# Prompt attention woven into the sample attention, V pages requested ahead of K pages, in a two-layer hybrid decoder step

## The chip, the cores and the metric

One NeuronCore of a Trainium2 chip runs the whole step as one program. The metric is device time in microseconds, the median of several executions. One further execution was profiled; all rows come from it.

## The reference, cut to what matters

A prompt of 512 tokens and a sample group of 8 sequences with 8 new tokens each (576 tokens, T) pass two decoder layers of width 1024, all in float32. Layer 0 mixes tokens by trailing mean pooling (256 channels) and by forgetting attention (12 heads of 64), layer 1 by gated spatial mixing and retention; each has an MLP of 4096 behind. The change touches layer 0's mixer alone:

```python
# prompt: causal, over its own 512 rows, logits biased by differences of the summed log gates
sc = einsum('bqhd,bkhd->bhqk', qb, k) * scale + cb[..., :, None] - cum[..., None, :]
p = softmax(where(kpos <= qpos, sc, -inf)); o = einsum('bhqk,bkhd->bqhd', p, v)
# samples: 8 queries of each sequence over 4096 past rows (32 pages of 128, by page_table) and 8 new ones
s_past = einsum('bqhd,bkhd->bhqk', q, k_past) * scale + g[..., :, None] + suffix[..., None, :]
p = softmax(concatenate([s_past, s_new])); o = p_past @ v_past + p_new @ v
```

The past keys and values are 256 pages of K and 256 of V, 384 KiB each, 201 MB in all. The pooling's new history rows, K, V and the log gates of the new tokens are outputs too.

## The kernel before

Activations lie with channels on the partitions, tokens along the free dimension (`big`, `xn`, `h`). Each engine has its own instruction list, in program order, and they meet by semaphores; SP issues the loads of weights and pages, GpSimd (POOL) those of small tables and the stores.

**Order of layer 0.** After the first norm come the ten column pairs of the input projection (`pairs("in", 0)`, a scheme of seven products, `seven`). Then TensorE transposes the cached log gates (`sfxT`) and sums them up (`sfx`), takes the new tokens' gates (`logfT`, `cum`, `cumT`), and turns K and V of the new tokens into rows (`knat`, `vnat`), which POOL stores (`k_stored`, `v_stored`). Then the **prompt attention**: 48 steps, 12 heads of 4 query blocks. Step n: `score` (L974, L975) of block i against i + 1 key blocks, with the gate as an extra row of staged queries and keys (`qz`, `kz`, filled by ScalarE's `queries` and small SP loads); VectorE's `maximum`, ScalarE's exponential, VectorE's `divisors` (a diagonal matrix of reciprocals), TensorE's `turn` (L985), ScalarE's copy, per head `weigh` (L996) and VectorE's `head_out`. It is pipelined over four score banks and three turning banks. POOL makes the pooling differences meanwhile. After it the pool outputs, then the sample attention.

**Sample attention.** The 32 pages of a sequence go in 4 groups of 8: 32 groups g. K pages go into a ring of 12 slots (4-page blocks), V pages into one of 8. VectorE transposes each K page in place (`turn_page`, L1898). `score_group(g)` (L1047) is 224 small matmuls that fill four banks; it starts when all eight pages are turned. VectorE takes the maximum (`shift_group`, L1913), ScalarE the exponential (L1462), TensorE transposes the probabilities (`turn_probs`), ScalarE copies them (L1477), TensorE weighs V pages 0 to 3 (`weigh_page`, L1069), and pages 4 to 7 behind the next score block. In TensorE's list, for each g:

```python
score_group(g)
if g: 
    for p in range(GP // 2, GP): weigh_page(g - 1, p)
turn_probs(g)
for p in range(GP // 2): weigh_page(g, p)
```

VectorE's list for g: `turn_pages(g + 1, 0..2)`, `shift_group(g)`, page 3, `add_out(g - 1)`, the bias, pages 4 to 7. SP's list runs through pages n in fours: K pages n to n+3 (L540, waiting for `scored` >= (n - 12) // 8 + 1 from page 12 on), then V pages n-8 to n-5 (L545, each waiting for `v_page_used` >= page - 7 from page 8 on). Two batches of page numbers are read into registers ahead of each such eight (L528).

The new tokens' own scores, `score_new`, `turn_new`, `weigh_new`, come once per sequence, and `turn_out`, `place_out` bring its result into `xn`. After the last group follows the output projection (`pairs("out", 0)`), whose two weight units were loaded into `wring` during the input projection.

Of the kernel before, what the change touches and what calls it, by code (L numbers as in the profile page):

```python
# [57 lines left out]
for _n, _k in PARAMS:  # L58
# [6 lines left out]
STAGES = [("x", KD), ("norm0", 1), ("logf", 1), ("sfxT", 12), ("logfT", 1), ("sfx", 6),  # L65
          ("cum", 1), ("knat", 5), ("cumT", 1), ("vnat", 5), ("hist", 2), ("g96", 1),
# [158 lines left out]
def hybrid_step(nc, I, O, where0, where1, decay_step):  # L225
    ctx = ExitStack()
    with ctx:
# [29 lines left out]
        kTn = sb("kTn", [TS, FOX])  # L257
# [23 lines left out]
        def bankB(s, n=TS, rows=P):  # L281
# [7 lines left out]
        vs = bigf[:, at0 + 3072:at0 + 3840]  # L289
        q4 = bigf[:, at0 + 3840:at0 + 5376].rearrange("p (n t) -> p n t", n=2 * H)  # L290
        qcur = bigf[:, at0 + 5376:at0 + 6912].rearrange("p (e c i f n) -> p e c i f n", e=2, c=CG, i=HC, f=2)
        key_bias, qgate = sbias[:, 0:TS], sbias[:, TS:TS + NB]
        at1 = EV_V * T
        es = [bigf[:, at1 + 1536 + 368 * n:at1 + 1536 + 368 * (n + 1)].rearrange("p (a b t) -> p a b t", a=2, b=NB)
              for n in range(2)]
        hstage = bigf[0:NB * HIST, at0 + 6408:at0 + 6664]
        hcopy = bigf[:, at1 + 2528:at1 + 2768].rearrange("p (a t) -> p a t", a=2)
        hout = bigf[0:NB * HIST, at1 + 2768:at1 + 3024]
        hout_p = bigf[0:HIST, at1 + 3024:at1 + 3280]
# [3 lines left out]
        probs = work[:, 9216:10240]  # L303
        pTs = work[:, 10240:11264].rearrange("p (g r) -> p g r", g=GP)
        bias_nat = work[:, 11264:11520].rearrange("p (g n) -> p g n", g=GP)
        bias_T = work[:, 11520:12032].rearrange("p (e n) -> p e n", e=2)
        out_acc = work[:, 12032:12416].rearrange("p (e n) -> p e n", e=2)
        v_ring = bigf[:, EV_Q * T:EV_Q * T + VSLOTS * FOX].rearrange("p (s n) -> p s n", s=VSLOTS)
        at3 = EV_Q * T + VSLOTS * FOX
        probs_new = bigf[:, at3:at3 + NB * TS].rearrange("p (b t) -> p b t", b=NB)  # L310
        pTn = bigf[0:TS, at3 + NB * TS:at3 + NB * TS + P]
        ostage = bigf[:, at1 + 1136:at1 + 1328]
        lg = work[:, 0:3072].rearrange("p (a s h) -> p a s h", a=2, h=H)
        kstage = work[:, 0:3840].rearrange("p (t n) -> p t n", t=NT + 1)
# [3 lines left out]
        vn0 = work[:, W2:W2 + NT * FOX].rearrange("p (t n) -> p t n", t=NT)  # L318
# [6 lines left out]
            .rearrange("p (s n) -> p s n", s=4)  # L325
        ngate = rstd[0:H, 0:SEQ]

        KZ = W1 + 1024 + 2 * EXT + 4 * P
        kz = [xn[:, KD - 1, 0:SEQ], work[:, KZ:KZ + SEQ]]

        def stat(b, n):
# [1895 lines left out]
```

## Time and profile before

| | |
|---|---|
| median of 3 runs (lowest, highest) | 2286.21 us (2284.81, 2288.41) |
| the profiled execution: time, span | 2289.08 us, 2287.2 us |
| busy: PE, VectorE, ScalarE, GpSimd | 87%, 47%, 15%, 9% of the span |
| input projection and what precedes it | 0 to 185.2 us |
| gates, K and V rows | 185.2 to 240.6 us |
| prompt attention and pool outputs | 240.6 to 358.7 us |
| sample attention: first page requested, block 0 done, block 31 done | 358.75, 380.8, 922.2 us |
| output projection begins | 936 us |
| read from memory, written | 309.2 MB, 8.55 MB |

Busy shares are means over stages with different limits, so they say little about one stage; the stage is cut out by windows, and in it one asks which wait ends last. In rows of the timeline "idle before <-releaser" is the time that the engine stood idle before the instruction, and what ended it.

### The profile page before, as it was taken

How to read it: one execution, taken by the hardware profiler on the slowest of the kernel's cores; microseconds unless marked ns; L12 is line 12 of the kernel's file. 1: busy time of each engine (PE TensorE's matmuls, PEld its weight loads, DVE VectorE, ACT ScalarE, POOL GpSimd, SP SyncE). 2: the span in 40 equal slices, each digit the busy share in tenths (PEclk: the TensorE clock that was granted, in tenths of full speed). 3: DMA queues.
4: the chain of work that ended last, by engine and by line, in shares of the span. 5: the costliest groups of instructions: out<-in, count | busy, mean ns of one | idle time of the engine just before them, and what ended most of it. 6: DMA issues, size and time to landing. Idle time of an engine off the chain costs nothing.

```text
span 2287.2 us, 40891 instructions
## 1 busy us (share of the span) xinstructions
PE 1981.6 (87%) x16723; PEld 1487.8 (65%) x16723; DVE 1064.5 (47%) x1915; ACT 354.2 (15%) x817; POOL 197.5 (9%) x266
## 2 busy tenths in 40 slices
PE   6999885666766666889999999999997899999996
PEld 4777663444444444667777777677775677777774
DVE  5331855565665565453334444232456533344443
ACT  2002451111111111112221000111011022210002
POOL 1000500000000000100001222100001100002221
PEclk9999997888788898999999999999898999999998
DMA  4221106999999999312222222222111222222221
GB/s 162 74 74 38 63 2 225 340 373 357 372 367 355 357 384 367 119 37 74 74 74 90 93 76 74 74 74 74 39 32 56 74 74 74 74 74 74 74 74 42
DMA packets 127990, 320.42 MB, mean 140 GB/s; under 512 B 10236, under 2 KB 10514, under 8 KB 127678
## 3 DMA queue, kind: packets, MB, share of 16 engines
q1 hardware_dynamic: 124258, 304.67, 36.4%
q0 software_dynamic: 3296, 12.98, 1.7%
q8 instruction: 134, 2.20, 0.4%
q14 instruction: 50, 0.41, 0.1%
q10 hardware_dynamic: 252, 0.16, 0.0%
HBM read 309.20 MB, written 8.55 MB: 139 GB/s over the span
## 4 chain that ended last, share of the span: by engine, by line
PE 76%; DVE 8%; DMA 6%; issue 5%; SPq 4%; ACT 1%; ACTq 0%; DVEq 0%
PE ps L847 49%; PE ps L1047 7%; DMA work<-in_cache_k 5%; DVE work L1898 3%; PE ps L1161 3%; PE ps L1162 3%; SPq L540 2%; PE ps L769 1%; PE ps L770 1%; PE ps L996 1%; SPq L545 1%; PE ps L798 1%; PE ps L799 1%; SPq L528 1%; PE ps L1069 1%
## 5 line engine op out<-in xcount | busy, mean ns | idle before, releaser
L1898 DVE STREAM_TRANSPOSE work<-work 128x768 f32<-128x768 f32 x256 | 245.2, 971 | 160.9 <-DMA work<-in_cache_k 160.1
L847 PE MATMUL ps<-xn,wring 128*128 128x288 f32 x1104 | 295.5, 411 | 20.0 <-DVE xn L1617 15.7
L847 PE MATMUL ps<-work 128*128 128x288 f32 x1152 | 296.5, 411 | 12.4 <-DVE work L1664 7.8
L847 PEld LDWEIGHTS ps<-work 128*128 128x128 f32 x1152 | 221.7, 193 | 75.6 <-issue 13.7
L847 PEld LDWEIGHTS ps<-xn,wring 128*128 128x128 f32 x1104 | 212.4, 193 | 80.7 <-issue 20.0
L847 PE MATMUL ps<-big,wring 128*128 128x288 f32 x944 | 251.4, 410 | 7.6 <-DVE big L2172 7.6
L1047 PE MATMUL ps<-work,big 32*32 32x256 f32 x6144 | 165.4, 471 | 92.2 <-DVE work L1898 61.6
L847 PEld LDWEIGHTS ps<-big,wring 128*128 128x128 f32 x944 | 181.0, 192 | 58.7 <-DVE big L2172 8.5
L1047 PEld LDWEIGHTS ps<-work,big 32*32 32x32 f32 x6144 | 113.9, 115 | 136.4 <-DVE work L1898 74.3
L1691 DVE TENSOR_TENSOR work<-ps,work 128x288 f32<-128x288 f32 x72 | 33.0, 458 | 320.1 <-PE ps L847 320.1
L702 POOL TENSOR_TENSOR h<-h,xn 128x288 f32<-128x288 f32 x96 | 106.1, 1108 | 812.4 <-DVE xn L1698 697.6
L1069 PE MATMUL ps<-big,work 128*32 128x192 f32 x2048 | 126.5, 394 | 48.1 <-ACT work L1477 32.0
L847 PE MATMUL ps<-work,wring 128*128 128x288 f32 x576 | 151.4, 406 | 0.0
L1069 PEld LDWEIGHTS ps<-big,work 128*32 128x32 f32 x2048 | 70.1, 128 | 97.8 <-ACT work L1477 39.3
L847 PEld LDWEIGHTS ps<-work,wring 128*128 128x128 f32 x576 | 109.4, 190 | 30.2
L1383 ACT ACTIVATE work<-ps 128x288 f32<-128x288 f32 x72 | 29.6, 411 | 622.0 <-PE ps L847 622.0
L847 PE MATMUL ps<-big,work 128*128 128x288 f32 x448 | 116.2, 406 | 0.0
L1462 ACT ACTIVATE work<-ps,stats 128x1024 f32<-128x1024 f32 x32 | 35.7, 1114 | 441.9 <-DVE stats L1915 441.9
L847 PEld LDWEIGHTS ps<-big,work 128*128 128x128 f32 x448 | 85.1, 190 | 23.5
L847 PE MATMUL ps<-xn,work 128*128 128x288 f32 x368 | 96.7, 406 | 0.0
L1161 PE MATMUL ps<-xn,wring 128*128 128x288 f32 x256 | 83.1, 406 | 0.0
L1162 PE MATMUL ps<-xn,wring 128*128 128x288 f32 x256 | 83.0, 406 | 0.0
(348 smaller groups left out, 2345.2 us busy)
## 6 DMA issues: line engine op xcount, KB each, us to landing
work<-in_cache_k SPq DMA_DIRECT2D x256, 384.0 KB, 5.9
big<-in_cache_v SPq DMA_DIRECT2D x256, 384.0 KB, 7.5
wring<-in_w_up SPq DMA_DIRECT2D x16, 2048.0 KB, 7.6
wring<-in_w_down SPq DMA_DIRECT2D x16, 2048.0 KB, 7.8
wring<-in_w_in_odd SPq DMA_DIRECT2D x6, 2048.0 KB, 8.1
wring<-in_w_in_even SPq DMA_DIRECT2D x5, 2048.0 KB, 9.1
wring<-in_w_out_even SPq DMA_DIRECT2D x2, 2048.0 KB, 8.4
wring<-in_w_out_odd SPq DMA_DIRECT2D x2, 2048.0 KB, 7.8
```

Of the source, the lines that this page charges most:

```text
L528: _, ids = nc.values_load_multi_w_load_instructions(ptab[0:1, n:n + 4], engines=[mybir.EngineType.SP], min_val=0, max_val=NPHYS - 1)
L540: sp.dma_start(k_ring[:, k_slot(n), :], rows_of("cache_k", page)).then_inc(k_in[k_slot(n)], 16)
L702: pool.tensor_tensor(hs[name], hs[name], xouts[kind, layer][:, g % 2, a, :], ALU.add)\
L847: last = mm(bank, w[:, k, :], x[:, k, :], start=k == 0 and not onto, stop=k == 3, skip_group_check=onto)
L1047: last = mm(ps[32 * c:32 * c + 32, 4 + q, 0:256], w, x, start=(n == 0), stop=(n == 2 * HC))
L1069: last = mm(ps[32 * c:32 * c + 32, 3, 0:HC * D], pTs[:, place(g, p), 32 * c:32 * c + 32], v_ring[:, n % VSLOTS, HC * D * c:HC * D * (c + 1 ...
L1161: mm(bankA(s, TH), w, xn[:, k, 0:TH], start=(k == 0), stop=(k == KD - 1))
L1162: last = mm(bankB(s, TH), w, xn[:, k, TH:T], start=(k == 0), stop=(k == KD - 1))
L1383: act_f(sums_at(g)[2][:, g % 2, :], ps[:, 4 * (g % 2), 0:TH], ACT.Copy).then_inc(sem("p1_copied"), 1)
L1462: act_f(probs.rearrange("p (g q k) -> p q g k", g=GP, q=4), ps[:, 4:8, 0:256].rearrange("p q (g k) -> p q g k", g=GP), ACT.Exp, bias=shift ...
L1691: ins = tt(u2, bank[1], first[:, g % 2, :], ALU.add)
L1898: nc.vector.transpose(x, x).then_inc(sem("k_turned"), 1)
```

## The change

- **The prompt's 48 steps are spread over the sample groups 0 to 23**, two a group, with the tail in group 24 (`prompt_step(2 * g)` between weighing V pages 4 to 7 and `turn_probs`, `prompt_step(2 * g + 1)` at the end of the group). One score bank, one turning bank, two exponential buffers take the place of four, three and four. Queries and keys are read from `big` directly, and the gate is a matmul of its own with a broadcast column of the identity; `queries` and the SP loads of the gate rows are gone. The queries are scaled in place by ScalarE during the input projection, and `place_queries` moves there.
- **Pages are requested from the end of `sfx` on.** In SP's list four V pages stand ahead of each four K pages. V page 0 waits for the K rows' stores and the turned new keys, since the V ring now lies in `wring`. The output projection's weights go into `big`, behind the last K page and a wait for the last prompt head.
- **Pooling moves ahead**: the history transposes come before the first norm's products, POOL's pooling runs under the input projection and writes its differences in place (`big`), the history outputs come right after the projection, the group matmuls (`pooled`) ahead of `g96`. ScalarE waits for `pool_d_ready` before it copies the gates' transposes.
- **TensorE waits for `v_stored` ahead of `score_new(0)`**; before it waited for it ahead of the same call, but behind the prompt attention. `score_group` also waits for `outputs_placed`. `stage_queries`, `score_new`, `shift_new` come one group earlier (GS - 3), `turn_new`, `weigh_new`, `start_out` half a group to a group earlier.

```diff
@@ SP
-            unit("out0", 0)
-            unit("out0", 1)
             sp.wait_ge(sem("ptab_in"), 16)
-            sp.wait_ge(sem("ngate_ready"), 1)
...
-            for hd in range(H):
...
-                sp.dma_start(kz[hd % 2][r:r + 1, :], ngate[hd:hd + 1, :]).then_inc(sem(f"gates_in_{hd % 2}"), 16)
-            sp.wait_ge(sem("fox_prompt_done"), H)
+            wait_emptied(sp, FIRST["sfx"] + 6)
...
             def v_page(n, page):
+                if n == 0:
+                    sp.wait_ge(sem("k_stored"), 80)
+                    sp.wait_ge(sem("new_keys_turned"), 1)
...
             for n in range(GP, NB * PAGES, 4):
                 k_ids, v_ids = page_ids(n), page_ids(n - GP)
                 for m in range(4):
+                    v_page(n - GP + m, v_ids[m])
+                for m in range(4):
                     k_page(n + m, k_ids[m])
-                for m in range(4):
-                    v_page(n - GP + m, v_ids[m])
+            sp.wait_ge(sem("fox_prompt_done"), H)
+            unit("out0", 0)
+            unit("out0", 1)
@@ TensorE
+            pe.wait_ge(sem("v_stored"), 32)
+            gates = rstd[:, 0:SEQ]
             def score(n):
...
+                if n:
+                    pe.wait_ge(sem("probs_made"), n)
+                w, r = (i + 1) * P, slice(64 * (hd % 2), 64 * (hd % 2) + 64)
+                mm(ps[:, 0, 0:w], big[r, EV_Q + hd // 2, i * P:w], big[r, EV_K + hd // 2, 0:w], start=True, stop=False)
+                mm(ps[:, 0, 0:w], ident[:, hd:hd + 1].broadcast_to([P, P]), gates[:, 0:w], start=False, stop=False)
+                mm(ps[:, 0, i * P:w], ident, cst("mask"), start=False, stop=True).then_inc(sem("scores_made"), 1)
...
+            def prompt_step(n):
+                if n >= NT + 1 and (n - 1) % NT == 0 and n <= NSTEP + 1:
+                    weigh((n - 1) // NT - 1)
+                if 1 <= n <= NSTEP:
+                    turn(n - 1)
+                if n < NSTEP:
+                    score(n)
...
             for g in range(NG):
                 b, new = g // GS, g // GS + 1
                 score_group(g)
+                if g % GS == GS - 2 and new < NB:
+                    turn_new(new)
                 if g:
                     for p in range(GP // 2, GP):
                         weigh_page(g - 1, p)
...
+                prompt_step(2 * g)
                 turn_probs(g)
...
                 for p in range(GP // 2):
                     weigh_page(g, p)
...
                 if g % GS == 0 and b:
                     turn_out(b - 1)
+                prompt_step(2 * g + 1)
@@ ScalarE
             for g in range(NG):
+                if 1 <= 2 * g - 1 < NSTEP:
+                    exp_prompt(2 * g - 1)
+                if 0 <= 2 * g - 2 < NSTEP:
+                    take_turned(2 * g - 2)
                 exp_group(g)
+                if 1 <= 2 * g - 1 < NSTEP:
+                    take_turned(2 * g - 1)
                 take_probs(g)
+                if 2 * g < NSTEP:
+                    exp_prompt(2 * g)
@@ VectorE
                 turn_pages(g + 1, range(0, 3))
+                if 1 <= 2 * g - 1 < NSTEP:
+                    divisors(2 * g - 1)
                 shift_group(g)
...
                 if g:
                     add_out(g - 1)
...
+                if 2 * g < NSTEP:
+                    maximum(2 * g)
+                if g % 2 == 1 and g >= 3 and g // 2 - 1 < H:
+                    head_out(g // 2 - 1)
+                turn_pages(g + 1, range(3, 4))
                 if g + 1 < NG:
                     turn_bias(g + 1)
...
+                turn_pages(g + 1, range(4, 5))
+                if 2 * g < NSTEP:
+                    divisors(2 * g)
+                turn_pages(g + 1, range(5, 8))
...
                 if g % GS == 0 and b:
                     place_out(b - 1)
+                if 2 * g + 1 < NSTEP:
+                    maximum(2 * g + 1)
```

## Rows read from the trace of the kernel before

**Rows 1.** The page, DMA share in tenths and GB/s in 40 equal slices.

```profile
DMA  4221106999999999312222222222111222222221
GB/s 162 74 74 38 63 2 225 340 373 357 372 367 355 357 384 367 119 37 74 74 74 90 93 76 74 74 74 74 39 32 56 74 74 74 74 74 74 74 74 42
```

**Rows 2.** Windows: us, busy PE, PEld, DVE, ACT, POOL, clock, DMA share, GB/s.

```profile
185.20:240.60 55.40, 49.91 (x204) 39.31 (x204) 14.91 (x36) 16.89 (x37) 9.68 (x16) 0.93 0.24 86
240.60:358.70 118.10, 102.99 (x538) 76.82 (x539) 72.67 (x226) 58.26 (x167) 23.96 (x31) 0.96 0.03 9
...
380.80:922.20 541.40, 353.71 (x9561) 230.82 (x9565) 325.02 (x541) 77.52 (x138) 11.65 (x60) 0.85 0.97 360
922.20:936.00 13.80, 7.55 (x108) 4.23 (x107) 6.74 (x20) 2.41 (x4) 0.00 (x0) 0.87 0.36 116
```

**Rows 3.** DMA queues, 381 to 922 us: packets, MB, share of 16 engines.

```profile
q1 hardware_dynamic: 70848, 193.49, 95.8%
```

**Rows 4.** Timeline, 374 to 390 us: start us, us, engine, line, operation.

```profile
379.80 0.99 PE L1047 MATMUL ps<-work,c 32*32 32x256 f32 x27
...
380.97 1.88 SPq L540 DMA_DIRECT2D work<-in_cache_k  x4
...
386.00 2.79 PE L1069 MATMUL ps<-big,work 128*32 128x192 f32 x32 [1.11 <-ACT work L1477]
387.13 1.97 DVE L1898 STREAM_TRANSPOSE work<-work 128x768 f32<-128x768 f32 x2 [0.47 <-DMA work<-in_cache_k]
...
389.15 1.24 PE L1047 MATMUL ps<-work,big 32*32 32x256 f32 x43 [0.36 <-DVE work L1898]
```

**Rows 5.** Timeline, 920 to 932 us, the end of the stage.

```profile
921.23 0.40 PE L1047 MATMUL ps<-work,big 32*32 32x256 f32 x1 [2.94 <-issue]
...
921.23 0.97 PE L1047 MATMUL ps<-work,c 32*32 32x256 f32 x32
...
930.67 0.53 PE L1069 MATMUL ps<-big,work 128*32 128x192 f32 x8 [0.41 <-DMA big<-in_cache_v]
```

**Rows 6.** SP queue's own waits, 381 to 922 us: us, times, longest.

```profile
SPq L540 <- PE ps L1047: 55.0, 24, 4.9
```

**Rows 7.** Line 540, requests of 380.9 to 382.9 us, time to landing.

```profile
DMA to landing us min/median/max: 2.9/4.6/5.6
```

**Rows 8.** Line 1047 alone, 374 to 922.2 us, columns as in Rows 2.

```profile
374.00:922.20 548.20, 191.42 (x7168) 131.28 (x7168) 0.85 0.96 358
```

**Rows 9.** Waits, 374 to 922.2 us: us in total, times, longest.

```profile
PE ps L1047 <- issue: 53.8, 24, 3.8
```

**Rows 10.** Lines, 240 to 358 us: busy us, mean ns, idle before.

```profile
L985 PE MATMUL ps<-work 128*128 128x128 f32 x240 | 36.7, 285 | 12.4 <-issue 8.0 <-DVE work L1850 3.4 <-ACT work L1442 0.8
...
L1850 DVE TENSOR_SCALAR work<-c,hstat 128x128 f32<-128x128 f32 x48 | 17.9, 372 | 1.8 <-DVE hstat L1849 0.2
L974 PE MATMUL ps<-work 128*128 128x128 f32 (+3 forms) x48 | 17.4, 444 | 0.0
```

**Rows 11.** Stretch of 386 to 388 us, columns as in Rows 2.

```profile
386.00:388.00 2.00, 2.00 (x28) 1.27 (x32) 1.53 (x2) 0.00 (x0) 0.00 (x0) 0.50 0.95 376
```

**Rows 12.** Timeline, three moments between 224 and 363 us.

```profile
224.22 1.08 ACT L1402 ACTIVATE big<-ps 128x512 f32<-128x512 f32 x1 [0.63 <-PE ps L922]
...
237.27 0.79 POOL L619 DMA_DIRECT2D out_v_prompt<-work  x1 [4.16 <-DVE work L1793]
...
237.84 0.45 DVE L1807 COPY big<-ps 128x120 f32<-128x120 f32 x2
...
362.75 0.83 PE L1082 MATMUL ps<-kTn,big 32*32 32x8 f32 x48 [3.31 <-DVE big L1890]
```

**Rows 13.** All DMA issues: KB each, median us to landing.

```profile
out_v_prompt<-work POOLq DMA_DIRECT2D x1, 1536.0 KB, 5.8
```

**Rows 14.** Line 1842, all of the run: ns min/median/max.

```profile
L1842 DVE SCALAR_TENSOR_TENSOR hstat<-hstat,cumn x48: 219/220/1877, 242.6 to 347.5; 128x1 f32<-128x1 f32 x48
```

**Rows 15.** Timeline of SP's queue, 150 to 230 us.

```profile
157.65 27.53 SPq L504 DMA_DIRECT2D wring<-in_w_out_even  x2
```

More of the change, by code:

```diff
@@ L484, in unit @@
                 u = UFIRST[stage] + j
-                if u >= 2:
+                if u >= 2 and stage != "out0":
                     for name, n, per in WEIGHTS:
@@ L816, in _ @@
             pe.wait_ge(sem("params_ready"), 1)
+            pe.wait_ge(sem("hist_in"), 16)
+            for a in range(2):
+                s = slot("hist", a)
+                open_block(FIRST["hist"] + a)
+                tr(ps[:, 2 * s, 0:NB * HIST], hstage[:, a * P:(a + 1) * P], ident[0:NB * HIST, 0:NB * HIST])\
+                    .then_inc(block_in, 1)
             s = slot("logf")
@@ L894, in _ @@
             pe.wait_ge(sem("c11_out_in"), c11_before(last_in + 1, "in"))
+            s = slot("hist_out")
+            for a in range(2):
+                tr(ps[0:NB * HIST, 2 * s + a, 0:P], hcopy[:, a, :], ident)
+                last = tr(ps[0:HIST, 2 * s + a, P:2 * P], hcopy_p[:, a, :], ident)
+            last.then_inc(block_in, 1)
             pe.wait_ge(sem("lg_in"), 32)
@@ L1716, in first_weight_sums, with place_queries, under_in @@
                     weight_sum(pairs_of(kind, layer)[0], name)
+            def place_queries(n):
+                a, f, q = n // 8, n // 4 % 2, n % 4
+                at = 64 * a + 32 * f
+                cp(q4[32 * q:32 * q + 32].rearrange("p (n a f) t -> p a f n t", a=2, f=2)[:, a, f],
+                   big[at:at + 32, EV_Q:EV_Q + HB, SEQ:T])
+            def under_in(g):
+                if g == 0:
+                    dve.wait_ge(sem("mixed"), MIX["C21"])
+                    for a in range(2):
+                        own(cp(es[0][:, a, :, HIST:HIST + NS], big[:, a, SEQ:T].rearrange("p (b s) -> p b s", b=NB)))
+                        cp(hcopy[:, a, :].rearrange("p (b t) -> p b t", b=NB), es[0][:, a, :, NS:NS + HIST])
+                    cp(hcopy_p, big[:, 0:2, SEQ - HIST:SEQ]).then_inc(sem("ext_ready"), 1)
+                if 5 <= g < 9:
+                    dve.wait_ge(sem("queries_scaled"), 3)
+                    for n in range(4):
+                        place_queries(4 * (g - 5) + n)
             def pairs(every, last=None):
@@ L1756, in _ @@
             first_weight_sums("in", 0)
+            for a in range(2):
+                s = drained("hist", a)
+                cp(es[0][:, a, :, 0:HIST], ps[:, 2 * s, 0:NB * HIST].rearrange("p (b t) -> p b t", b=NB))\
+                    .then_inc(out_of["vector"], 1)
             norm(0, PROW["norm_mix"], 0)
@@ L1770, in _ @@
             act_sum(0, "T4")
-            pairs(pairs_of("in", 0))
+            pairs(pairs_of("in", 0), under_in)
             dve.wait_ge(sem("c11_out_in"), c11_before(pairs_of("in", 0)[-1] + 1, "in"))
+            nc.vector.memset(rstd[:, :], 0.0).then_inc(sem("gates_zeroed"), 1)
+            s = drained("hist_out", 0)
+            for a in range(2):
+                cp(hout[:, a * P:(a + 1) * P], ps[0:NB * HIST, 2 * s + a, 0:P])
+                last = cp(hout_p[:, a * P:(a + 1) * P], ps[0:HIST, 2 * s + a, P:2 * P])
+            last.then_inc(out_of["vector"], 1)
+            wait_emptied(dve, FIRST["hist_out"] + 1)
+            dve.sem_inc(sem("hist_out_ready"), 1)
             dve.wait_ge(sem("log1p_ready"), 1)
@@ L1930, in shift_new @@
                 x = probs_new[:, b, NS * b:NS * b + NS]
-                own(tt(x, new_psum[:, 0:NS], key_bias[:, NS * b:NS * b + NS], ALU.add))
+                own(tt(x, ps[:, 2, 320:320 + NS], key_bias[:, NS * b:NS * b + NS], ALU.add))
                 own(nc.vector.reduce_max(neg_max(b, 0), x, AX.X, negate=True))
```

377 lines of the change are left out of this document (144 added, 233 removed).

## The prediction, made before the changed kernel was run

> **What bounds the kernel now.** I read the page first. Its DMA row is at 9 tenths over slices 8 to 16 of 40 and at 2 almost everywhere else [rows 1]. That names one stage in which memory is the limit: the sample attention, which streams 512 cache pages of 384 KiB. So I cut the span into stages. The prompt attention, 240.6 to 358.7 us, moves 9 GB/s. The sample attention between its first and its last finished score block, 380.8 to 922.2 us, moves 360 GB/s at a DMA share of 0.97 [rows 2], 95.8% of it the SP queue's packets [rows 3]. The two do not overlap: one stage has no traffic, the next has little else. That is what interleaving could win, at most about 118 us.
>
> The second question is whether the pages come at 360 GB/s whatever the order of the requests. One group is 16 pages (6.29 MB) and takes (922.20 - 380.79) / 31 = 17.46 us [rows 4, 5]. At 360 GB/s 16 pages take 17.47 us, so the rate sets it. But SP also waits 55.0 us in 24 places for `scored`, the end of a score block [rows 6]: there is a closed loop (scores of group g end, K pages are requested, land, are transposed, scores of g+1 run), and its slack is small. One turn of this loop from an empty queue is visible, because DMA ran dry before the first block ended: block 0 ends at 380.79, SP requests four K pages at 380.97, they land 2.9 to 5.6 us after their requests [rows 7], DVE turns the last one by 389.10, block 1 starts at 389.15 [rows 4]. That is 8.36 us from one block's end to the next one's start. A block itself takes (191.42 busy + 53.8 idle inside it) / 32 = 7.66 us [rows 8, 9]. Loop from empty: 8.36 + 7.66 = 16.0 us, against 17.46. So the present order leaves 1.4 us a group, which shows as requests queued. This is the number on which the change turns.
>
> **What the change does to the loop.** The new SP order puts four V pages ahead of each four K pages. In steady state the V pages ahead of the K half that group g+1 lacks are the second half of group g. Their ring slots come free only when `weigh_page(g-1, 4..7)` runs, which TensorE does right after score block g. So these requests can't be sent early: when block g ends, SP sits at a V request, sends four V, then the four K. The loop gains four pages. A page is 393 KB; at 360 GB/s 1.09 us, so 4.3 us, and about 0.4 us until the first page is weighed (32 records take 2.79 us at the lower clock [rows 4]). Gap 8.36 + 4.3 + 0.4 = 13.1 us; period 13.1 + 7.66 = 20.7 us. This exceeds 17.5 us, so the queue runs empty each turn and no backlog hides it. The second halves (V of g+1, K of g+2) go out at about 8 us and are through by 20 us; they just don't add. From both sides: not below the rate's 17.5 us; above, the four K pages from idle came 1.4 us apart (from 380.97 + 2.9 = 383.9 to about 388.1), and four more at that pace are 5.6 us: 22.0 us. I take 20.7, since that spacing fell in the first microseconds after idle, when little was under way.
>
> The Trainium skill (DMA: Bandwidth & Descriptors, Bandwidth) puts the limit of a core from memory at about 358 GB/s; the trace's 360 agrees. By that rule alone the order of requests is free and the period stays 17.5 us; that is the first rival below.
>
> **Prompt work inside the loop** (two steps a group, groups 0 to 23). TensorE: the prompt stage's PE busy time is 102.99 us [rows 2]; over 24 groups 4.3 us. The gates are now a matmul of their own over the score's width, 48 of them at the 444 ns of a score matmul [rows 10] or somewhat more (the records come in pairs): 0.9 to 1.8 us a group. The sample stage has 353.71 / 31 = 11.4 us busy a group [rows 2]. Together 17 us of a 20.7 us period: it fits, but little is free. Step 2g lies between the V weighing and `turn_probs`, where TensorE waits for the maximum and the exponential: hidden at the full clock. Step 2g+1 must end before block g+1. It waits for `divisors(2g)`, which VectorE now does behind `turn_page` 4, so behind a landing at about 9 us: the step ends at 11.5 to 13 us, abreast of the pages. VectorE: `divisors` (372 ns [rows 10] and a reciprocal) stands between transposes of the last pages and delays them by 0.5 us, the rest is done while it waits for pages. When a block stalls and the granted clock drops to 0.5, as at 386 us [rows 11], weighing and step 2g take twice as long. I take 0.5 us a group for both: period 21.2 us. In seven groups the next block also waits for `place_out` (about 0.6 us).
>
> Sum over the 31 periods: the first has no V slot to wait for (18.9 us), 23 at 21.2 = 487.6, 7 at 20.7 = 144.9, 7 x 0.6 = 4.2: 655.6 us against 541.4. **+114 us.**
>
> **The start.** The anchor is `score_new(0)`, at 362.75 us before [rows 12]. It now waits for `v_stored`. The V store is issued at 237.27 us [rows 12] and lands in 5.8 us [rows 13] with no other traffic. Before it come now the output transposes of the history (four 128x128 matmuls, with 285 ns each [rows 10] 1.1 us), two history copies ahead of the first norm (0.45 us [rows 12]), and the pooling on GpSimd, which moves under the input projection. Beside it a VectorE instruction of 220 ns once took 1.88 us [rows 14]; between 0 and 6 us in all, I take 2. The store also runs beside the first K and V pages, now requested from about 227 us (the suffix sums are copied out at 225.3 [rows 12]): I double its 5.8 us. 237.3 + 3.6 + 11.6 = 252.5, so **-110 to -111 us** (bounds -116 without contention, -106 with more). The Trainium skill (DMA: Bandwidth & Descriptors, Queues, rings and completion order) says that each DMA engine serves its queues in turn by packets; by that rule the store gets half the engines' time, the same doubling; no row here shows it. Block 0 then follows 18 us later as before (380.8 - 362.75): its pages are long there. Pooling, its matmuls and scaling, the query scaling on ScalarE and `place_queries` lie under the projection, TensorE's stage, or under the wait for the store: nothing; without that cover a few us.
>
> **The end.** The two weight units of the output projection (4 MiB, 11.6 us at 360 GB/s) were loaded at 157.65 us [rows 15]; now they stand between the last K and the last eight V pages. After block 30: 8 pages, 4 MiB, 8 pages, that is 26.7 pages, the last landing near 0.6 + 2.9 + 25.7 x 1.09 = 31.5 us, or 10.8 us after block 31 ends. Before, the last weighing started 8.5 us after it (930.67 - 922.20) [rows 5]. **+3 us** with its spread. The stages behind are unchanged.
>
> **Sum.** The profiled execution has 2289.1 us: -111 + 114 + 3 = +6, so 2295; it lies 2.9 above the median, so **2293 us** in the runs' terms: the hidden prompt attention is given back almost exactly by the loop.
>
> **Rivals.**
> *A. The rate hides the order.* If the V slots come free early enough, or landings overlap more, the period stays 17.5 us and only the start counts: 2286 - 111 + 3 = 2178 us. For it: share 0.97 and the match with 360 GB/s. Against it: `weigh_page(g-1, 4..7)` is behind block g in TensorE's own order, and the loop from empty has 1.4 us of slack for 4.7. Chance 0.10.
> *B. Score blocks get shorter.* 53.8 of their time is idle put down to issue [rows 9], and clock is lost after such stalls. If TensorE, kept busy or waiting longer ahead of a block, runs it in 191.42 / 32 = 6.0 us, periods are 19.5 and 19.1 us: 602 us, +60, 2286 - 111 + 60 + 3 = 2238 us. For it: the idle time lies in 24 places of 32 blocks, so some blocks run without. Against: the last block still waited 2.94 us [rows 5], after more waiting than the others. Chance 0.20.
> *C. TensorE becomes the bound,* the other side. 17 us of work with three waits in series (exponential, copy, `divisors`) at a lower clock: if step 2g+1 ends at 15.3 us instead of 13, it decides (from 13.6 us on). Period 23 us in 24 groups: 697 us, +155, 2286 - 111 + 155 + 3 = 2333 us. Chance 0.15.
> *Main case,* 0.55: 2270 to 2318 us (a period half a us shorter or longer is 16 us).
>
> **How the numbers follow.** What a measurement here can tell from no change is 0.2%, 4.6 us: 2281.6 to 2290.8 is the same. Faster: A, B and 0.07 of the main case, 0.37. Same: 0.11. Slower: C and 0.37 of the main case, 0.52. Signs of both kinds hold much, so the range is wide: 2235 to 2335 leaves out A and the far parts of B and C, 0.2 together. The upper bound of the period (22.0 for 20.7 us, 40 us in all: 2333) lies inside.
>
> **What the profile after will show.** Block 0 ends near 270 us. Score block ends 20 to 21.5 us apart, in the last seven groups too, where there is no prompt work: this tells the loop from C. The DMA share there near 0.83 and 300 GB/s. SP waits at the V request (L545's line) for the weighing, many times 3 to 6 us, and hardly at the K request. Wrong would be: share 0.95 and above with ends 17.5 us apart (A); blocks of 6 us (B); long groups only until the twenty-fourth (C); a block 0 after 280 us (the store).

## The result: slower by 1.7%, inside the range

The changed kernel takes 2326.66 us (median of 4 runs, 2325.02 to 2330.91), the kernel before, beside it, 2287.31 us (2284.81 to 2291.41). The ratio is 1.0173, 95% interval 1.0152 to 1.0194: slower by 39 us, where +6 to +7 us was forecast. Sign and range (2235 to 2335) hold; the size does not, and the time lies above the 2270 to 2318 us of the main case. The profiled execution has a span of 2323.5 us against 2287.2, +36.3 us. It splits at the first and the last finished score block, read off the timeline:

| | before | after | difference | forecast |
|---|---|---|---|---|
| block 0 ends | 380.79 | 270.49 | -110.3 | -111 |
| from there to the end of block 31 | 541.4 | 686.6 | +145.2 | +114 |
| rest of the span | 1365.0 | 1366.4 | +1.4 | +3 |

So start and end are right within 2 us and the whole error, 31 us, lies in the 31 periods. The page of the kernel after, DMA share in tenths and GB/s in 40 slices, to be laid beside [rows 1]:

```profile
DMA  4210777868878778611222222321211112222221
GB/s 159 73 37 14 282 282 272 304 249 299 302 274 293 276 283 306 223 73 50 96 73 73 73 73 73 109 73 37 75 31 56 72 63 82 73 73 73 73 73 41
```

The plateau begins earlier and is longer, but it never reaches 9. The windows of the kernel after (columns as in [rows 2]) say the same by stage. With `score_new(0)` at 250.90 us, block 0's end at 270.4 and the end of the prompt steps near 780 us:

```profile
250.90:270.40 19.50, 8.89 (x282) 6.07 (x282) 11.01 (x17) 1.68 (x3) 0.39 (x2) 0.54 0.50 196
270.40:780.00 509.60, 398.43 (x7726) 256.12 (x7720) 295.65 (x602) 99.15 (x241) 8.88 (x46) 0.89 0.78 283
780.00:950.00 170.00, 99.24 (x2316) 64.56 (x2313) 85.17 (x144) 22.16 (x41) 2.71 (x14) 0.78 0.80 293
```

A DMA share of 0.78 to 0.80 stands against 0.97 in [rows 2] (0.83 and 300 GB/s were forecast), and it is as low in the last seven groups, where there is no prompt work at all. The limit is no longer the rate. What took its place is in the waits of SP's own queue, 270 to 900 us (us in total, times, longest), which answer to [rows 6]:

```profile
SPq L533 <- PE ps L1045: 203.2, 37, 9.5
SPq L525 <- PE ps L1023: 17.4, 1, 17.4
```

Line 533 is the V request, line 1045 `weigh_page`. The wait at the K request (line 525) has all but gone: SP stands at V pages instead. One group without prompt work shows the loop. Block 25 ends at 824.78 us (timeline, columns as in [rows 4]):

```profile
825.45 1.88 SPq L533 DMA_DIRECT2D wring<-in_cache_v  x4
...
827.51 2.03 SPq L525 DMA_DIRECT2D work<-in_cache_k  x4
...
834.67 3.82 DVE L1857 STREAM_TRANSPOSE work<-work 128x768 f32<-128x768 f32 x4 [5.54 <-DMA work<-in_cache_k]
...
838.55 5.42 PE L1023 MATMUL ps<-work,big 32*32 32x256 f32 x187 [6.54 <-DVE work L1857]
```

and the landing of the four K requests of 827.5 to 829.1 us after their issue:

```profile
DMA to landing us min/median/max: 7.1/7.8/8.4
```

Against the loop from empty in [rows 4, 7]: the K requests go out 2.7 us after the block's end, not 0.2, and take 7.8 us, not 4.6, to land. The gap is 13.8 us where it was 8.36. The window from the first of these eight requests to the landing of the last K page (825.45 us to 829.1 + 8.4; columns as in [rows 2]) and, below it, the landing of the four V requests that follow at 832.75 us:

```profile
825.45:837.51 12.06, 3.87 (x108) 2.60 (x100) 6.35 (x11) 2.41 (x4) 0.39 (x2) 0.91 0.92 332
DMA to landing us min/median/max: 5.7/6.4/7.1
```

332 GB/s over 12.06 us are 4.0 MB, 10.2 pages, though the block waits for eight only. The other 2.2 belong to the four later V pages, none of which has landed by then.

In a group with prompt work something else ends the gap. Block 13 ends at 558.33 us. TensorE's next step 2g+1 and block (same view, TensorE, the transposes and `divisors`):

```profile
568.20 0.98 DVE L1857 STREAM_TRANSPOSE work<-work 128x768 f32<-128x768 f32 x1 [2.45 <-DMA work<-in_cache_k]
...
569.26 0.29 DVE L1836 TENSOR_SCALAR big<-c,hstat 128x128 f32<-128x128 f32 x1
...
569.65 1.62 PE L980 MATMUL ps<-big 128*128 128x128 f32 x6 [2.81 <-issue]
...
569.90 2.89 DVE L1857 STREAM_TRANSPOSE work<-work 128x768 f32<-128x768 f32 x3 [0.35 <-DMA work<-in_cache_k]
...
571.20 2.07 PE L968 MATMUL ps<-big 64*128 64x512 f32 x2
...
573.20 2.08 PE L969 MATMUL ps<-rstd,c 128*128 128x512 f32 x2
...
575.07 0.63 PE L970 MATMUL ps<-c 128*128 128x128 f32 x2
...
575.63 4.56 PE L1023 MATMUL ps<-work,big 32*32 32x256 f32 x183
```

The pages are turned at 572.79 us, but the block waits 2.8 us more for the step, which runs at the lower clock level (1.2 GHz, granted clock 0.50; columns as in [rows 2]) after TensorE had stood still for 2.8 us. (The row names issue for it, but the wait ends 0.1 us after `divisors`, line 1836, and so it does in 20 of the 24 prompt groups.)

```profile
569.60:575.60 6.00, 5.95 (x12) 3.02 (x12) 3.44 (x6) 0.39 (x2) 0.00 (x0) 0.50 1.02 393
575.60:581.00 5.40, 5.32 (x226) 3.46 (x225) 4.08 (x7) 1.16 (x3) 0.00 (x0) 0.98 0.30 115
```

The second row is the other side of it: TensorE comes to the block from work instead of from a wait, at the upper clock level (2.4 GHz, granted clock 0.98), and this block takes 5.4 us; the mean before was 7.66. The Trainium skill (TensorE: Matmul & The Clock Gate, HAM oscillation — how this bites in real kernels) says that waits for data between short bursts of matmuls bring the clock down again each time; the trace agrees in this turn, with 0.50 after the wait of 2.8 us.

### The profile page after: what moved, and what is told of

Its sections match the earlier page's. It is cut to its first block, busy times and chain, and to the rows that moved or that the text cites. A ratio compares the mean times of both kernels' runs of the same rounds, so it can differ in the third digit from the quotient of the medians.

```text
span 2323.5 us, 41057 instructions
## 1 busy us (share of the span) xinstructions
PE 2030.2 (87%) x16827; PEld 1506.5 (65%) x16827; DVE 1057.5 (46%) x1915; ACT 342.9 (15%) x796; POOL 196.2 (8%) x260
## 4 chain that ended last, share of the span: by engine, by line
PE 80%; DMA 7%; DVE 6%; issue 4%; SPq 2%; ACT 1%; ACTq 0%; POOL 0%; DVEq 0%
PE ps L837 48%; PE ps L1023 8%; DMA work<-in_cache_k 5%; PE ps L1140 3%; PE ps L1141 3%; PE ps L1045 3%; DVE work L1857 2%; PE ps L969 1%; PE ps L752 1%; PE ps L968 1%; PE ps L753 1%; SPq L533 1%; PE ps L781 1%; PE ps L980 1%; PE ps L782 1%
## 5 line engine op out<-in xcount | busy, mean ns | idle before, releaser
L837 PE MATMUL ps<-xn,wring 128*128 128x288 f32 x1008 | 268.9, 410 | 16.7 <-DVE xn L1593 15.7
L837 PEld LDWEIGHTS ps<-xn,wring 128*128 128x128 f32 x1008 | 193.4, 192 | 71.8 <-issue 16.5
L1045 PE MATMUL ps<-wring 128*32 128x192 f32 x2048 | 113.5, 363 | 42.4 <-ACT wring L1445 35.6
L837 PE MATMUL ps<-work,wring 128*128 128x288 f32 x544 | 143.0, 406 | 0.0
L837 PEld LDWEIGHTS ps<-work,wring 128*128 128x128 f32 x544 | 103.4, 190 | 28.6
L1045 PEld LDWEIGHTS ps<-wring 128*32 128x32 f32 x2048 | 65.9, 120 | 84.0 <-ACT wring L1445 43.4
L1140 PE MATMUL ps<-xn,wring 128*128 128x288 f32 x256 | 83.1, 406 | 0.0
L1141 PE MATMUL ps<-xn,wring 128*128 128x288 f32 x256 | 83.0, 406 | 0.0
L837 PEld LDWEIGHTS ps<-xn,work 128*128 128x128 f32 x368 | 69.9, 190 | 19.3
```

Of the source, the lines that this page charges most:

```text
L837: last = mm(bank, w[:, k, :], x[:, k, :], start=k == 0 and not onto, stop=k == 3, skip_group_check=onto)
L1045: last = mm(ps[32 * c:32 * c + 32, 3, 0:HC * D], pTs[:, place(g, p), 32 * c:32 * c + 32], v_ring[:, n % VSLOTS, HC * D * c:HC * D * (c + 1 ...
L1140: mm(bankA(s, TH), w, xn[:, k, 0:TH], start=(k == 0), stop=(k == KD - 1))
L1141: last = mm(bankB(s, TH), w, xn[:, k, TH:T], start=(k == 0), stop=(k == KD - 1))
```

## Experiments

All kernels ran beside runs of the kernel before (medians of 2289 to 2293 us); differences between two of them are taken from the ratios. "Period" is the distance of score block ends in the profiled execution, periods 2 to 24 (prompt work, where there is any) and the last 7. "Block" is the mean length of the 32 score blocks, the gap what lies between two of them.

| kernel | us | ratio and 95% interval | period 2-24 / last 7 | block |
|---|---|---|---|---|
| before | 2287 | 1 | 17.5 / 17.2 | 7.66 |
| changed kernel | 2327 | 1.0173 [1.0152, 1.0194] | 22.5 / 22.0 | 6.89 |
| e1 interleaved, K ahead | 2257 | 0.9860 [0.9826, 0.9895] | 20.4 / 18.1 | 7.46 |
| e2 stages apart, V ahead | 2416 | 1.0549 [1.0513, 1.0586] | 21.6 / 21.2 | 7.58 |
| e3 all V weighed earlier | 2281 | 0.9960 [0.9935, 0.9985] | 21.1 / 20.0 | 7.12 |
| e4 V ahead, no prompt steps | 2309 | 1.0087 [1.0053, 1.0122] | 21.8 / 21.6 | 7.62 |
| e5 K ahead, no prompt steps | 2199 | 0.9585 [0.9551, 0.9620] | 18.0 / 17.7 | 8.01 |
| e6 stages apart, V V K K K K V V | 2359 | 1.0296 [1.0261, 1.0330] | 19.9 / 19.4 | 7.82 |
| e7 e1, head weighed in a wait | 2253 | 0.9828 [0.9798, 0.9858] | 20.4 / 18.0 | 7.84 |
| e8 e4 with twelve V slots | 2198 | 0.9593 [0.9564, 0.9621] | 18.2 / 18.0 | 7.73 |
| e9 K pages half turned | 2315 | 1.0101 [1.0081, 1.0122] | 22.1 / 21.6 | 7.32 |
| e10 e7 without gates | 2243 | 0.9766 [0.9723, 0.9808] | 20.2 / 17.8 | 7.27 |
| e11 e7 without bias | 2198 | 0.9591 [0.9567, 0.9614] | 18.2 / 17.1 | 5.94 |
| e12 e7, bias in four matmuls | 2229 | 0.9728 [0.9702, 0.9753] | 19.3 / 17.1 | 6.81 |

**e1, e2: the order alone, in both arrangements.** e1 is the changed kernel with the old order of requests, e2 the kernel before with the new one.

```diff
                 for m in range(4):
-                    v_page(n - GP + m, v_ids[m])
-                for m in range(4):
                     k_page(n + m, k_ids[m])
+                for m in range(4):
+                    v_page(n - GP + m, v_ids[m])
```

> The interleaved kernel with the one order undone: four K pages ahead of each four V pages, all else as changed. Theory L (the four V requests wait for the weighing behind the score block and so lengthen the loop by their transfer): the 4.3 to 5 us go, the period falls from 22.15 to 17.5 to 19.5 us, SP no longer waits long at the V request, time 2190 to 2245 us. Theory C (the prompt work makes TensorE the bound, the order matters little): period stays above 21 us, time 2290 us or more.

> The kernel before with the SP order alone changed to four V pages ahead of four K pages; the prompt attention stays in a stage of its own. Theory L: gap 13 to 14.5 us plus a block of 7.7 us, period 21 to 22.2 us against 17.46, time 2286 + 31 x (3.6 to 4.7) = 2395 to 2432 us. Theory C: there is no prompt work in the groups, so the period stays near 17.5 and the time within 10 us of 2287.

V ahead costs +126 us in the old arrangement (ratio 1.0549) and +72 us in the new one (1.0173 - 0.9860). Interleaving alone, with K ahead, is faster than before by 32 us. e2 lies inside its interval; e1 lies above the 2190 to 2245 us of theory L, and far below the 2290 of theory C: the loop is gone, and something else is there. e1's queue waits lie at the K request again (381 to 900 us):

```profile
SPq L525 <- PE ps L1023: 103.6, 22, 8.0
SPq L533 <- PE ps L1045: 2.7, 7, 1.4
```

Yet e1 does not run at the rate: 20.4 us a period with prompt work. TensorE has no wait for pages there: all 24 blocks of the prompt groups start at once behind the step before. One of them (timeline of e1):

```profile
563.70 1.51 PE L1045 MATMUL ps<-wring 128*32 128x192 f32 x32 [1.11 <-ACT wring L1445]
565.13 2.42 PE L992 MATMUL ps<-big,work 128*128 128x512 f32 x8
567.39 0.39 PE L980 MATMUL ps<-big 128*128 128x128 f32 x2
...
569.18 3.95 PE L1023 MATMUL ps<-work,big 32*32 32x256 f32 x184
575.91 0.42 PE L1023 MATMUL ps<-work,big 32*32 32x256 f32 x4 [2.78 <-issue]
```

Step follows step; the one hole, 2.78 us inside the block, is put down to issue. The DMA queues show what comes at that moment (573.1 to 574.6 us: packets, MB, share of 16 engines):

```profile
q1 hardware_dynamic: 212, 0.58, 99.0%
q8 instruction: 1, 0.02, 4.3%
```

Queue 8 brings instructions, 16 KiB a packet, while the page queue (q1) keeps the DMA engines 99% busy. This packet ends at 574.58 us and the hole 1.33 us later. So it is with every hole of 1 us or more inside a score block in all fourteen traces: 258 of them, each ending 1.17 to 1.66 us after a packet of queue 8 has ended. Such a packet comes every 7.7 us here, so chance would put some 8% of the holes there.

**e3: the V slots freed before the block.** All eight V pages of a group are weighed before step 2g+1 instead of four after the next block.

```diff
                 score_group(g)
-                if g:
-                    for p in range(GP // 2, GP):
-                        weigh_page(g - 1, p)
...
-                for p in range(GP // 2):
+                for p in range(GP):
                     weigh_page(g, p)
...
-            for p in range(GP // 2, GP):
-                weigh_page(NG - 1, p)
```

> The changed kernel with V still requested ahead of K, but TensorE weighs all eight V pages ahead of prompt_step(2g + 1), none behind the next score block, so that the V slots come free some 10 us before the block ends and SP's V requests go out then. Theory L: the K half is the first thing requested when a block ends, the period falls to 17.5 to 20 us, time 2185 to 2260 us. Theory C: TensorE has as much to do and more of it ahead of the block, period 22 us or more, 2320 us or more. If it is the bytes of V ahead of K in the queue, and not the moment of their request, that cost, the period stays near 22 us too.

-49 us against the changed kernel, with V ahead all the same, but above the 2185 to 2260 us that I had expected. SP's wait splits into line 525, 85.5 us, and line 533, 70.3 us (28 and 38 times, 270 to 900 us), so the loop is shorter, not gone. That the weighing now has to wait for V pages that were requested late is my reading; no run tests it.

**e4, e5: without the prompt's attention** (its 48 steps, and the waits for them, are left out), with V and with K ahead.

```diff
-        NSTEP = H * NT
+        NSTEP = 0
...
-            sp.wait_ge(sem("fox_prompt_done"), H)
```

> The changed kernel with all 48 prompt steps left out (the prompt's attention is not computed, its rows of the output projection's input hold older values). Theory L: the loop does not need them, period 21 to 22.2 us in all groups, time 2295 to 2326 us. Theory C: the period falls to 17.5 to 18.5 us, time 2180 to 2215 us.

> Interleaved, K pages ahead of V pages, and no prompt steps (the prompt's attention is left out). With e1 (2257 us, period 19.8), with the changed kernel (2327, 22.15) and with the changed kernel without prompt steps (2309, 21.5) this closes a square of four: order of requests by prompt work. Theory L (two loops: requests held at V slots; and TensorE's own work, 16 to 17 us a group with the prompt steps): with K pages ahead and no prompt steps neither loop decides, the period is the rate's 17.5 to 17.9 us, the last block ends near 815 us, total 2185 to 2195 us; so the prompt steps cost 60 to 70 us with K pages ahead but only 17 us with V pages ahead. Rival: the interleaved arrangement has a cost of its own in both orders (about 0.7 us a group, as the steps cost with V ahead): period 19 and above, 2235 to 2245 us.

This closes a square. The steps cost 0.0086 (20 us) with V ahead and 0.0275 (63 us) with K ahead; V ahead costs 0.0502 (115 us) without steps and 72 us with them. The two limits don't add: while the loop waits for pages, TensorE's extra work mostly fits in the wait. The arrangement itself costs little (e5: 18.0 us a period, the kernel before 17.5). e4 lies inside its interval, e5 4 us above its own.

**e6: half the dose.** The kernel before with two V pages ahead of the four K pages.

```diff
+                for m in range(2):
+                    v_page(n - GP + m, v_ids[m])
                 for m in range(4):
                     k_page(n + m, k_ids[m])
-                for m in range(4):
+                for m in range(2, 4):
                     v_page(n - GP + m, v_ids[m])
```

> The kernel before with two V pages ahead of the four K pages and two behind (V V K K K K V V). The dose of e2 halved. Theory L: each V page ahead of the K pages adds its transfer, 1.09 us, to the loop; from e2's 21.4 us two pages less give 19.2 us: (19.2 - 17.46) x 31 = +54, 2335 to 2350 us. Rival: what costs is that SP's queue stands still until the block ends, however many V pages are ahead: 2400 to 2420 us as in e2.

2359 us, above my interval by 9, but far from e2's. The mean gap between blocks (without the first) tells more: 9.8 us in the kernel before, 12.0 with two V pages ahead, 14.0 with four. The first pair costs 2.2 us and the second 2.0, some 1.0 us a page, as the transfer time says.

**e8: free slots.** e4 with twelve V slots; the four new ones lie in the prompt's V, which nothing reads without the steps.

```diff
-KSLOTS, VSLOTS = 12, 8
+KSLOTS, VSLOTS = 12, 12
...
+        def v_slot(n):
+            s = n % VSLOTS
+            return v_ring[:, s, :] if s < 8 else vn0[:, s - 8, :]
...
+                if n == 8:
+                    sp.wait_ge(sem("v_stored"), 32)
```

> The changed kernel (V ahead) without prompt steps (left out), with 12 slots for V pages instead of 8: the four new ones lie where the prompt's V was kept, which nothing reads without the steps. A V page now waits for the weighing of the page twelve before it, that is of the first half of a group, which is done long before the next score block ends. Theory L: the order V, K costs only through the slots that come free behind the score block; with free slots the requests run ahead, the period falls from 21.5 to 17.5 to 18 us and the total from 2309 to 2185 to 2205 us. Rival: V pages ahead of K pages cost by being ahead, whether their slots are free or not (they take the engines' time first): period above 20, 2270 us and more.

-113 us against e4, and level with e5 (0.9593 and 0.9585), with V still ahead of K. This is the cleanest result of the study: being ahead costs nothing; what costs is a request at the head of an in-order queue whose slot comes free behind the block. It is shown without prompt work; with it, no run had twelve slots. SP's waits in e8 hold no row for a V request (270 to 900 us; L529 is the K request, L509 the weights of a later stage):

```profile
SPq L529 <- PE ps L1028: 92.4, 26, 18.1
SPq L509 <- PE ps L842: 47.3, 1, 47.3
```

**e9: half of each transpose** on the changed kernel; half of the keys stay unturned.

```diff
-                x = k_ring[:, slot, :]
+                x = k_ring[:, slot, 0:FOX // 2]
```

> The changed kernel with each K page transposed over half its width only (half of the keys stay unturned; requests, waits and matmuls are the same). In the changed kernel the four K pages that gate a block land nearly together, and their four transposes of 0.97 us run one behind the other up to the next block's start. If this series is the missing microsecond of the loop, the gap falls by about 1.9 us a group: 31 x 1.9 = 59, 2327 to about 2268 us (2260 to 2280). If the last landing alone sets the start, only the last transpose counts: 0.5 x 31 = 15, 2305 to 2315 us.

-16 us by the ratios (half-width about 7): the theory of four transposes in series falls. In the last seven groups the gap goes from 14.1 to 13.8 us, less than the half transpose of the last page; the last landing sets it.

**e7, e10, e11, e12: what bounds the groups with K ahead.** e7 moves a head's four weighing matmuls of e1 into TensorE's wait for ScalarE's copy:

```diff
-                if n >= NT + 1 and (n - 1) % NT == 0 and n <= NSTEP + 1:
-                    weigh((n - 1) // NT - 1)
...
                 turn_probs(g)
+                if g % 2 == 0 and 1 <= g // 2 <= H:
+                    weigh(g // 2 - 1)
                 for p in range(GP // 2):
                     weigh_page(g, p)
```

e10 leaves out the gates' matmul of a prompt score (line 969):

```diff
-                mm(ps[:, 0, 0:w], ident[:, hd:hd + 1].broadcast_to([P, P]), gates[:, 0:w], start=False, stop=False)
```

e11 leaves out the 16 bias matmuls of a score block's 112:

```diff
-                for n in range(2 * HC + 1):
+                for n in range(2 * HC):
```

e12 computes all, with the bias in four matmuls of 32x128 weights:

```diff
-                for n in range(2 * HC + 1):
+                for n in range(2 * HC):
...
+                for q in range(4):
+                    r = slice(32 * q, 32 * q + 32)
+                    last = mm(ps[:, 4 + q, 0:256], head_row[r, 0:P], bias_T[r, g % 2, :], start=False, stop=True)
```

> e1 (K ahead) with the weighing of a head (four matmuls, 1.1 us at the full clock) taken out of prompt step 2g+1 and put between turn_probs and the weighing of the pages, where TensorE waits 1.1 us a group for ScalarE's copy. Twelve groups have it. If TensorE's work in series is what bounds the prompt groups of e1: -10 to -15 us against e1's 2257, 2240 to 2248 us. If the arrival of the pages bounds them: no change, 2253 to 2260 us.

> e7 (2252.5 us, K pages ahead) without the 48 matmuls that add the gates in the prompt's scores (that term is left out; 4 instructions of some 675 a group, about 1 us of TensorE's time). If the prompt groups of e7 are bound by TensorE's matmul time in series: 24 x 1.0 us, 2226 to 2232 us. If they are bound by the rate at which TensorE gets its instructions (waits put down to issue, 46 of 300 us): no change beyond 3 us, 2248 to 2254 us.

> e7 without the 16 matmuls of a score block that add the bias (that term is left out): one seventh of a block's matmuls, 32 instructions of some 675 a group, about 0.85 us of TensorE's time in 6.0 busy. By matmul time: 24 x 0.85 and little in the last groups, 2228 to 2235 us. By instructions: 32 / 675 of 20.2 us is 0.96 us a group, 2226 to 2234 us. Both give the same here; beside e10 it tells: if e10 moves nothing and e11 does, instructions are the bound; if both move alike, matmul time is; if neither, something else (pages) is.

> e7 (K pages ahead, 2252.5 us) with the bias of a score block added by 4 matmuls of 32x128 weights instead of 16 of 32x32: the whole computation is kept, the columns that run through the array are the same for each of the four row groups, and 12 matmuls a block less mean 48 records less (each matmul has two, each with its load) of some 672 a group. After e11 (all 16 left out, 64 records: -54 us) and e10 (8 records, but 1.7 us a group of busy time: only -9 us) I expect by the instruction count 48 / 672 x 20.2 = 1.4 us a group, 24 groups: -35 us, 2210 to 2225 us. Rival: what e11 saved was the time of the columns, which stay here: 2245 to 2256 us.

e7: -7 us with a half-width of 10, no clear gain, and 2252.5 us lies between the two intervals that I had set. Its window of 300 to 750 us shows why moving is not saving (waits of TensorE: us in total, times, longest):

```profile
PE ps L1021 <- issue: 56.0, 20, 4.0
PE ps L1043 <- ACT wring L1445: 12.2, 11, 1.1
PE ps L1043 <- issue: 8.5, 4, 2.4
```

The wait for the copy fell from 24.5 us (e1) to 12.2, but the waits put down to issue rose from 55 to 64. The groups by line, same window of e7 (busy us, mean ns, idle before), first the gates, then the bias:

```profile
L969 PE MATMUL ps<-rstd,c 128*128 128x512 f32 (+3 forms) x90 | 37.3, 497 | 0.0
...
L1021 PE MATMUL ps<-big,c 32*32 32x256 f32 x704 | 36.0, 470 | 15.8 <-issue 15.8
```

and the bias in e12:

```profile
L1020 PE MATMUL ps<-big,c 32*128 32x256 f32 x192 | 21.6, 512 | 2.1 <-issue 2.1
```

A matmul has two records, each with a load. Per group, gates: 1.66 us busy, 8 of about 672 records; bias: 36.0 / 22 = 1.64 us busy, 64 records; bias in e12: 21.6 / 24 = 0.90 us busy, 16 records, 48 fewer. My expectation for e11 counted its 16 matmuls as 32 records and was half too small; it came out 28 us below its interval, and e10 and e12 each lie between the two intervals set for them. Redone from these rows, what the period of groups 2 to 24 should lose against e7's 20.41 us:

| | by busy time | by record count | measured |
|---|---|---|---|
| e10 | 1.66 | 0.24 | 0.23 |
| e12 | 0.74 | 1.46 | 1.11 |
| e11 | 1.64 | 1.94 | 2.18 |

In whole times: e10 -14 us (half-width 12), e12 -23 (9), e11 -54 (9). The count fits all three, but for e10 the fit proves nothing. The windows of e7 and of e10 (columns as in [rows 2]):

```profile
300.00:750.00 450.00, 367.90 (x7579) 237.83 (x7579) 285.51 (x586) 97.36 (x235) 8.49 (x44) 0.93 0.86 312
300.00:750.00 450.00, 369.58 (x7560) 238.79 (x7556) 285.15 (x589) 97.59 (x235) 8.56 (x44) 0.87 0.86 314
```

and the mask's matmuls, the same 90 in both (line 970 in e7, line 969 in e10):

```profile
L970 PE MATMUL ps<-c 128*128 128x128 f32 x90 | 17.6, 277 | 0.0
...
L969 PE MATMUL ps<-c 128*128 128x128 f32 x90 | 24.4, 357 | 0.0
```

Without the gates the granted clock is 0.87 instead of 0.93, and matmuls of the same shape take longer. TensorE is busy for 369.58 / 450 x 20.18 = 16.6 us a period, and for 16.7 in e7, although 1.66 us of work is gone: the lower clock takes back nearly all of it. Why the clock is lower there is open.

e11 and e12 keep e7's clock of 0.93, and there the saving can be placed. From e7 to e12, the matmul time of a group's block falls by 0.1 us only; the waits at its lines put down to issue fall from 56.0 us to 35.7, about 1 us a group and nearly the whole gain:

```profile
PE ps L1016 <- issue: 33.6, 16, 3.3
PE ps L1020 <- issue: 2.1, 1, 2.1
```

These are the holes that end behind an instruction packet (see e1). e7 loads 134 such packets in the run, e12 128 and e11 126, and inside their blocks stand 24, 15 and 13 holes of 1 us or more. In e11 the same waits give 1.3 of the 2.2 us. So what the removed matmuls save is, for the larger part, waiting for TensorE's instructions; one profile each. Why a packet comes late, whether it stands behind page data for one, no run shows. The Trainium skill (TensorEngine Tiling (Array Packing), Performance Considerations, Instruction Overhead) knows a fixed price per matmul, which would also make fewer matmuls cheaper; the 0.1 us leaves little room for it here.

e12 keeps the whole computation: 2228.7 us, 2.7% faster than before and 4.4% faster than the changed kernel (0.9728 / 1.0173 = 0.956).

## Why the prediction was right, and where it was off

**Start (-110.3, forecast -111).** The waits are the right ones, the hit to 1 us is luck. `score_new(0)` starts at 250.90 us, forecast 252.5, and waits for the store as said (timeline):

```profile
250.90 0.82 PE L1059 MATMUL ps<-kv_new,big 32*32 32x8 f32 x48 [10.59 <-DMA out_v_sample<-kv_new]
```

Block 0 follows 19.6 us later, not 18, so two errors of 1.6 us cancel. Which of the small terms made them was not tested.

**The mechanism of the loop is right.** The wait moved from the K to the V request; the long groups go on to the end; e2 has the loop without any prompt work; e8 takes away the late slots, and the loss is gone. The waits are 203.2 / 37 = 5.5 us on average, as forecast (3 to 6), but up to 9.5.

**The size of a period failed.** Forecast were 655.6 us as 18.9 + 23 x 21.2 + 7 x 20.7 + 4.2; measured 14.7 + 23 x 22.51 + 7 x 22.02 = 686.6. Of the +31, the prompt groups give 23 x 1.31 = 30.1, the last seven 7 x 1.32 = 9.3, the first period gives back 4.2, and so does the term for `place_out`, since the measured periods hold it. The 18.9 us of the first period stood without a working; block 1, of 4.65 us, made it 14.7. The step that failed is "Gap 8.36 + 4.3 + 0.4 = 13.1 us". Without prompt steps the gap is 14.0 us (e4; e2 too), 0.9 more, in each of 30 periods 27 us. e6 places it: from two to four V pages the gap rises by 2.0 us, as 2 x 1.09 says; from none to two it rises, against the 8.36 us of [rows 4], by 3.7 instead of 2.6. The added pages were thus priced about right, and the base was too short, a loop measured when DMA had been idle. e9 excludes the transposes. In the group at 824.78 eight pages land in 12.06 us, the first after 3.0 us: 1.3 us a page, where I had taken 1.09 and set aside the 1.4 seen at block 0 (1.4 for all pages was my upper bound, 22.0 us a period; e4 has 21.8). The transfer is not slow there: the window above moves 10.2 pages in that time. In e4 the mean of 30 turns is 9.5 pages for the eight that the block waits for. "The second halves go out at about 8 us [...]; they just don't add" put this at nothing: in the group at 824.78 they go out at 8.0 us, as said, while the block's own pages are on the way until 12.7, and part of the engines' time goes to them. At 1.09 us a page 1.5 pages are 1.6 us, more than the 0.9 that are missing. No run held the second halves back, so how much of the 0.9 us is theirs is not shown.

The block's 7.66 us held in e4 (7.62) by luck: against the kernel before, the holes inside a block fell from 1.7 to 1.0 us and the matmul time rose from 6.0 to 6.7, at a granted clock of 0.77 for 0.85 over the stage.

**Prompt work.** Forecast +0.5 us a group; measured 22.51 - 21.82 (e4) = 0.7. The small sum hides two larger terms. The gap grows by 1.8 us (15.8 against 14.0), because step 2g+1 starts behind `divisors` and ends after the pages, often at the lower clock: rival C's mechanism. The block shrinks by 1.1 us (6.6 against 7.7). That is matmul time alone, 5.6 us instead of 6.7, at a granted clock of 0.88 instead of 0.72 inside these blocks: TensorE comes to them from work. Rival B had a shorter block for another reason, the holes; they are 1.0 us a block in both. The two terms cancel for the most part. Neither rival came at its price: 22.5 us is near C's 23 and 2327 us near its 2333, but the last seven groups have 22.0 us, and C can't act there.

**Rival A** is refuted as stated, and e8 shows when it would have held: with free slots the period is 18.0 to 18.2 us with V ahead, some 0.6 us above the kernel before. The Trainium skill's limit of about 358 GB/s (DMA: Bandwidth & Descriptors, Bandwidth) holds for the stage's mean in [rows 2]; the stretch at 569.6 us above moved 393 GB/s for 6 us, so for short stretches it is no ceiling; there the measurement decides.

**What I did not see.** The forecast treated interleaving and order as one sum and called the hidden prompt attention "given back by the loop". That is true of this kernel, but e1 shows a second limit behind the first: with the loop mended, TensorE's own series of 20.4 us, 16.5 of them matmuls and the rest idle, takes its place, and of the some 110 us hidden at the start only 32 arrive. My 17 us of TensorE work a group had left out the holes put down to issue, (56.0 + 8.5) / 22 = 2.9 us a group in e7, and [rows 9] had shown them: 53.8 us, for whose cause I did not ask.

## What to carry to other kernels

In a queue that issues requests in order, put first the requests whose slots are free at that time; ask of each request which instruction frees its slot and where that stands in its engine's order. Either the order (e1) or slots enough (e8) takes the loop away.

When a loop sets the period, measure its turn in steady state: a turn read where the queues had run empty was 0.9 us too short here, times 30. And work hidden in one limit's slack must be priced again once that limit is mended: the same prompt steps cost 20 us with V ahead and 63 us with K ahead.

In blocks of many small matmuls, count instructions as well as columns: a bias added by 4 matmuls instead of 16 gave 23 us. When TensorE stands still and the profile says issue, look for a packet of the instruction queue just before the end of the hole.

Before you conclude from a matmul left out, compare the granted clock of the two traces: e10's saving was taken back by a lower one.

## What the runs showed of the hardware

A score block of the same 112 matmuls (224 records) takes 4.65 us at the least and over 10 at the most (e5: 4.7 to 11.2). Part of it is the clock, part are holes put down to issue, and each hole of 1 us or more, 258 in fourteen traces, ended 1.17 to 1.66 us after a 16 KiB packet of the instruction queue. Their length depends on the kernel: 1.7 to 2.4 us a block in the kernel before, e1, e5, e7 and e8 (single holes up to 4.9), 0.8 to 1.0 in e2, e4 and the changed kernel, where late V slots leave the DMA engines idle for a fifth of the time (share 0.78 to 0.80; none over 2.4 in e4). Without the 16 bias matmuls the mean block falls from 7.84 to 5.94 us; the shortest, without holes, from 4.65 to 4.01.

Requests from idle queues land within 2.9 to 5.6 us [rows 7]; the K requests behind four V requests took 7.1 to 8.4 at 824.78 us.
